# A two-layer streaming encoder in float32: the second layer's panels computed without the meta-token columns that no output depends on

## The reference

```
def trunk_layer(x, pos, attend, sc_hist, cf_hist, ffn_hist, p):
    xn = rmsnorm(x, p['norm1_g'])
    q, k, v, sc_b, sc_c, sc_h, cf_a, cf_gate, gate_pre = jnp.split(xn @ p['w_in'], IN_SPLITS, axis=-1)
    ...
    y_attn = y_attn @ p['w_attn_out']
    sc_conv, new_sc = causal_dwconv(sc_c * sc_h, sc_hist, p['sc_conv_w'])          # width 3
    y_sc = (sc_b * sc_conv) @ p['w_sc_out']
    glu = cf_a * jax.nn.sigmoid(cf_gate)
    cf_conv, new_cf = causal_dwconv(glu, cf_hist, p['cf_conv_w'])                  # width 31
    y_cf = jax.nn.silu(layernorm(cf_conv, p['cf_ln_g'], p['cf_ln_b'])) @ p['w_cf_out']
    g_attn, g_sc, g_cf = jnp.split(jax.nn.sigmoid(gate_pre + p['b_gate']), 3, axis=-1)
    x = x + (g_attn * y_attn + g_sc * y_sc + g_cf * y_cf) @ p['w_o']
    h = rmsnorm(x, p['norm2_g']) @ p['w_up']
    h, new_ffn = causal_dwconv(h, ffn_hist, p['ffn_conv_w'])                       # width 3
    hg, hu = jnp.split(h, 2, axis=-1)
    return x + (jax.nn.silu(hg) * hu) @ p['w_down'], ...

y_prompt = rmsnorm(xp, final_g)[:, N_META:]        # the 16 meta tokens are dropped
y_sample = rmsnorm(xs, final_g)
```

## Time and profile before

| | us |
|---|---|
| median of 3 runs | 2459.11 (2457.91 to 2459.72) |
| profiled execution, its own time | 2460.99 |
| span of its trace, first to last instruction | 2459.7 |
| TensorE busy | 2390.1 (97%) |
| VectorE busy | 1616.4 (66%) |
| ScalarE busy | 891.3 (36%) |
| TensorE's granted clock, mean | 0.992 of full speed |

### The profile page before, as it was taken

One profiled execution on the slowest core, in us unless ns is written; L12 is line 12 of the kernel. 1 busy time (PEld: TensorE's weight loads), 2 busy tenths in 40 slices (PEclk: granted clock), 3 DMA queues, 4 the chain that ended last, 5 costly groups with the idle time before them and its releaser, 6 DMA issues.

```text
span 2459.7 us, 41837 instructions
## 1 busy us (share of the span) xinstructions
PE 2390.1 (97%) x17698; PEld 2342.4 (95%) x17698; DVE 1616.4 (66%) x2393; ACT 891.3 (36%) x1704; POOL 41.5 (2%) x73
## 2 busy tenths in 40 slices
PE   7999999999999999999999999999999999999997
PEld 6988899999999999999998889999999999999996
DVE  6577698895535664645764777988864356556366
ACT  4355322223523432423434562222244234234243
POOL 2000000000000000000010000000000000000000
PEclk9999999999999999999999999999999999999998
DMA  5311222222332222222242112222223322222222
GB/s 195 93 44 52 65 78 86 79 78 78 96 103 88 81 78 81 83 78 86 90 141 69 52 45 75 85 78 86 78 78 95 100 86 79 85 78 85 79 78 93
DMA packets 58284, 206.30 MB, mean 84 GB/s; under 512 B 8494, under 2 KB 8590, under 8 KB 57838
## 3 DMA queue, kind: packets, MB, share of 16 engines
q1 hardware_dynamic: 54704, 191.56, 24.0%
q0 software_dynamic: 3392, 12.05, 1.7%
HBM read 192.09 MB, written 8.50 MB: 82 GB/s over the span
## 4 chain that ended last, share of the span: by engine, by line
PE 89%; DVE 6%; ACT 2%; issue 2%; DMA 0%; SPq 0%; DVEq 0%; ACTq 0%
PE ps L386 86%; DVE cf_acc L1016 1%; PE ps L430 1%; DVE w_lo L825 1%; PE ps L443 1%; PE ps L462 1%; ACT w_hi L574 1%; PE ps L466 0%; DVE xn_hi_lo L873 0%; PE ps L398 0%; ACT scratch L657 0%; ACT L651 0%; ACT L601 0%; DVE scratch L869 0%; PE ps L448 0%
## 5 line engine op out<-in xcount | busy, mean ns | idle before, releaser
L386 PE MATMUL ps<-xn_hi_lo,w_hi 128*128 128x304 f32 (+1 forms) x7552 | 1358.5, 302 | 20.6 <-DVE w_lo L825 12.8
L386 PEld LDWEIGHTS ps<-xn_hi_lo,w_hi 128*128 128x128 f32 x7552 | 1122.7, 189 | 39.2 <-issue 27.3
L386 PE MATMUL ps<-xn_hi_lo,w_lo 128*128 128x304 f32 x3776 | 821.9, 299 | 0.0
L825 DVE TENSOR_TENSOR w_lo<-raw,w_hi 128x1024 fp32r<-128x1024 f32 x348 | 426.2, 1225 | 543.2 <-ACT w_hi L574 543.2
L574 ACT ACTIVATE w_hi<-raw 128x1024 fp32r<-128x1024 f32 x348 | 369.0, 1060 | 1121.2 <-PE ps L386 1120.7
L386 PEld LDWEIGHTS ps<-xn_hi_lo,w_lo 128*128 128x128 f32 x3776 | 609.2, 189 | 0.0
L386 PE MATMUL ps<-branch_hi_lo,w_hi 128*128 128x304 f32 (+1 forms) x2944 | 523.1, 300 | 3.8 <-DVE branch_hi_lo L1161 1.6
L386 PEld LDWEIGHTS ps<-branch_hi_lo,w_hi 128*128 128x128 f32 x2944 | 436.2, 188 | 6.7 <-DVE branch_hi_lo L1161 2.1
L1016 DVE SCALAR_TENSOR_TENSOR cf_acc<-glu,vec,cf_acc 128x622 f32<-128x622 f32 x480 | 382.8, 861 | 0.0
L386 PE MATMUL ps<-branch_hi_lo,w_lo 128*128 128x304 f32 x1472 | 318.9, 298 | 0.0
L386 PEld LDWEIGHTS ps<-branch_hi_lo,w_lo 128*128 128x128 f32 x1472 | 236.1, 188 | 0.0
(11 more groups left out here) (123 smaller groups left out, 1293.2 us busy)
## 6 DMA issues: line engine op xcount, KB each, us to landing
raw<-in_weights SPq DMA_DIRECT2D x348, 512.0 KB, 3.4
spill<-x_q_merged POOLq DMA_DIRECT2D x2, 2368.0 KB, 9.4
x_q_merged<-spill POOLq DMA_DIRECT2D x16, 296.0 KB, 3.2
x_q_merged<-in_xt SPq DMA_DIRECT2D x4, 592.0 KB, 8.7
out_y<-x_q_merged SPq DMA_DIRECT2D x8, 296.0 KB, 2.2
scratch<-scratch SPq DMA_DIRECT2D x72, 18.5 KB
scratch<-scratch SPq DMA_DIRECT2D x8, 132.0 KB, 2.3
con<-in_consts SPq DMA_DIRECT2D x1, 592.0 KB, 12.1
```

What stands on the lines that cost most here:

```text
L386: last = nc.tensor.matmul(to[:, t0:t1], a[:, w % 2, wk], both[:, part, k, t0:t1], start=(k == 0 and j == 0), stop=(k == nk - 1 and j == 2))
L825: V.tensor_tensor(wl[:, w % 2, :], raw[:, w % 2, :], f(wh[:, w % 2, :]), ALU.subtract).then_inc(lo_done, 1)
```

## The change

A function `lead(l, n)` gives, for each panel, the number of leading columns that are left out. In the first layer and ahead of the first gate panel it is 0. Behind that it is 16 for the down-projections, 12 for the short convolution's C and h panels, whose product the width-3 convolution reads two columns back, and 14 for all others. The front half's matmul and the operations of ScalarE and VectorE that read a panel out of PSUM or make its successor's input start at that column. Taps, layer norm, the feed-forward's convolution and SiLU, the channel sums and the final norm keep all columns. Number and order of the instructions on each engine, the semaphores and the transfers are as before.

```diff
--- before.py
+++ after.py
@@ -116,6 +116,19 @@
 
 
 USES = tile_uses()
+
+
+def lead(l, n):
+
+    if l < DEPTH - 1 or n < N_OA:
+        return 0
+    if N_SC <= n < N_OS and (n - N_SC) % 3 < 2:
+        return N_META - 2 * S_H
+    return N_META if any(p0 + 2 * k <= n < p0 + 2 * k + KT for t0, k, p0 in PARTS) else N_META - S_H
+
+
+def pieces(first):
+    return (first, TP - first), (TP, DEC_SEQ)
 
 
 def after(t0, hist):
@@ -382,7 +395,7 @@
                 pe.wait_ge(lo_done, w + 1)
             wk, to = slice(k * 128, k * 128 + 128), ps((l, n))
             for j, (a, part) in enumerate(((wh, 0), (wh, 1), (wl, 0))):
-                for t0, t1 in ((0, FRONT), (FRONT, TOK)):
+                for t0, t1 in ((lead(l, n), FRONT), (FRONT, TOK)):
                     last = nc.tensor.matmul(to[:, t0:t1], a[:, w % 2, wk], both[:, part, k, t0:t1],
                                             start=(k == 0 and j == 0), stop=(k == nk - 1 and j == 2))
             if k == nk - 1:
@@ -598,7 +611,8 @@
         def gate(l, n, j, bias):
 
             act.wait_ge(panel_done, l * PANELS + n + 1)
-            nc.scalar.activation(slot(O_SG, TOK, j), ps((l, n)), ACT.Sigmoid, bias=bias) \
+            t = lead(l, n)
+            nc.scalar.activation(slot(O_SG, TOK, j)[:, t:], ps((l, n))[:, t:], ACT.Sigmoid, bias=bias) \
                 .then_inc(out[USES[(l, n)][0]], 1)
 
         for m in range(KT):
@@ -717,11 +731,13 @@
                 if m >= 2:
                     tile_emptied(act, (l, n - 5))
                 act.wait_ge(panel_done, W + n + 1)
-                nc.scalar.activation(slot(O_CT, TOK, m % 2), ps((l, n)), ACT.Copy).then_inc(out[USES[(l, n)][0]], 1)
+                t = lead(l, n)
+                nc.scalar.activation(slot(O_CT, TOK, m % 2)[:, t:], ps((l, n))[:, t:], ACT.Copy).then_inc(out[USES[(l, n)][0]], 1)
                 high(W + n + 3)
                 high(W + n + 4)
                 tile_emptied(act, (l, n + 2))
-                nc.scalar.activation(bh[:, m, :], slot(O_BT, TOK, m % 2), ACT.Copy).then_inc(sc_hi, 1)
+                t = lead(l, n + 2)
+                nc.scalar.activation(bh[:, m, t:], slot(O_BT, TOK, m % 2)[:, t:], ACT.Copy).then_inc(sc_hi, 1)
 
             def mean(m):
                 act.wait_ge(sum_ps, l * 4 + 2)
@@ -767,7 +783,8 @@
                 high(W + N_OC + 2 * m + 3)
                 act.wait_ge(mg_done, l * 16 + 8 + m + 1)
                 act.wait_ge(tails_out, l * 32 + 32)
-                nc.scalar.activation(mh[:, m, :], X[:, m, :], ACT.Copy).then_inc(mg_hi, 1)
+                t = lead(l, N_WO)
+                nc.scalar.activation(mh[:, m, t:], X[:, m, t:], ACT.Copy).then_inc(mg_hi, 1)
             residual(l, N_WO, (l, l * 27 + 18, "g2"))
             root(l * 4 + 4, (l, "n2"), TOK, O_RF)
             act.wait_ge(ff_zero, l * 4 + 4)
@@ -842,11 +859,12 @@
             V.scalar_tensor_tensor(xl[:, m, :], X[:, m, :], col(l, g, m), f(xh[:, m, :]), ALU.mult, ALU.subtract) \
                 .then_inc(nx_lo, 1)
 
-        def conv3(src, dst, l, name, t, signal, base):
-            V.tensor_scalar(dst, src[:, 0:S_OUT], col(l, name, t * 3), None, ALU.mult).then_inc(signal, 1)
+        def conv3(src, dst, l, name, t, signal, base, first):
+            dst = dst[:, first:]
+            V.tensor_scalar(dst, src[:, first:S_OUT], col(l, name, t * 3), None, ALU.mult).then_inc(signal, 1)
             for k in (1, 2):
                 dve.wait_ge(signal, base + k)
-                V.scalar_tensor_tensor(dst, src[:, k:k + S_OUT], col(l, name, t * 3 + k), dst, ALU.mult, ALU.add) \
+                V.scalar_tensor_tensor(dst, src[:, first + k:k + S_OUT], col(l, name, t * 3 + k), dst, ALU.mult, ALU.add) \
                     .then_inc(signal, 1)
 
         zero_sum(O_SS, TOK)
@@ -1032,7 +1050,8 @@
                 low(W + N_OA + 2 * m + 3)
                 tile_emptied(dve, (l, N_OA + 2 * m))
                 dve.wait_ge(panel_done, W + N_OA + 2 * m + 2)
-                V.tensor_tensor(X[:, m, :], slot(O_SG, TOK, m % 2), ps((l, N_OA + 2 * m + 1)), ALU.mult) \
+                t = lead(l, N_OA)
+                V.tensor_tensor(X[:, m, t:], slot(O_SG, TOK, m % 2)[:, t:], ps((l, N_OA + 2 * m + 1))[:, t:], ALU.mult) \
                     .then_inc(out[USES[(l, N_OA + 2 * m + 1)][0]], 1)
                 taps(3)
 
@@ -1048,7 +1067,7 @@
                 low(W + n + 3)
                 tile_emptied(dve, (l, n))
                 dve.wait_ge(panel_done, W + n + 2)
-                for t0, w_ in PIECES:
+                for t0, w_ in pieces(lead(l, n + 1)):
                     o = after(t0, S_H)
                     last = V.tensor_tensor(ch[:, o:o + w_], slot(O_CT, TOK, j)[:, t0:t0 + w_],
                                            ps((l, n + 1))[:, t0:t0 + w_], ALU.mult)
@@ -1056,24 +1075,27 @@
                 tile_emptied(dve, (l, n + 1))
                 V.tensor_copy(sct[:, m, 0:S_H], ch[:, TP:TP + S_H])
                 V.tensor_copy(sct[:, m, S_H:2 * S_H], ch[:, S_IN - S_H:S_IN]).then_inc(sc_tail_done, 1)
-                conv3(ch, cv, l, "scw", m, sc_tap, (l * KT + m) * 3)
+                conv3(ch, cv, l, "scw", m, sc_tap, (l * KT + m) * 3, lead(l, n + 2))
                 taps(2)
                 low(W + n + 4)
                 dve.wait_ge(panel_done, W + n + 3)
                 dve.wait_ge(sc_tap, (l * KT + m) * 3 + 3)
-                for t0, w_ in PIECES:
+                for t0, w_ in pieces(lead(l, n + 2)):
                     o = t0 + (S_H if t0 >= TP else 0)
                     last = V.tensor_tensor(bt[:, t0:t0 + w_], cv[:, o:o + w_], ps((l, n + 2))[:, t0:t0 + w_], ALU.mult)
                 last.then_inc(out[3], 1)
                 taps(2)
                 dve.wait_ge(sc_hi, l * KT + m + 1)
-                V.tensor_tensor(bl[:, m, :], bt, f(bh[:, m, :]), ALU.subtract).then_inc(sc_lo, 1)
+                t = lead(l, n + 2)
+                V.tensor_tensor(bl[:, m, t:], bt[:, t:], f(bh[:, m, t:]), ALU.subtract).then_inc(sc_lo, 1)
 
             def merge(m, n, nth):
                 j = m % 2
-                V.tensor_tensor(slot(O_TQ, TOK, j), slot(O_SG, TOK, j), ps((l, n)), ALU.mult).then_inc(out[USES[(l, n)][0]], 1)
+                t = lead(l, n)
+                V.tensor_tensor(slot(O_TQ, TOK, j)[:, t:], slot(O_SG, TOK, j)[:, t:], ps((l, n))[:, t:], ALU.mult) \
+                    .then_inc(out[USES[(l, n)][0]], 1)
                 tile_emptied(dve, (l, n))
-                V.tensor_tensor(X[:, m, :], X[:, m, :], slot(O_TQ, TOK, j), ALU.add).then_inc(mg_done, 1)
+                V.tensor_tensor(X[:, m, t:], X[:, m, t:], slot(O_TQ, TOK, j)[:, t:], ALU.add).then_inc(mg_done, 1)
 
             def tile_sum(m):
                 ss = view(O_LS, CF_OUT)
@@ -1132,7 +1154,8 @@
                 dve.wait_ge(panel_done, W + n + 2)
                 merge(m, n + 1, 8)
                 dve.wait_ge(mg_hi, l * KT + m + 1)
-                V.tensor_tensor(ml[:, m, :], X[:, m, :], f(mh[:, m, :]), ALU.subtract).then_inc(mg_lo, 1)
+                t = lead(l, N_WO)
+                V.tensor_tensor(ml[:, m, t:], X[:, m, t:], f(mh[:, m, t:]), ALU.subtract).then_inc(mg_lo, 1)
 
             def residual(n0, following=None):
                 for m in range(KT):
@@ -1140,7 +1163,9 @@
                     if following is None or following[2] == "g2":
                         if n0 == N_WO:
                             dve.wait_ge(x_back, l * (KT * 16) + m * 16 + 16)
-                    V.tensor_tensor(X[:, m, :], X[:, m, :], ps((l, n0 + m)), ALU.add).then_inc(out[USES[(l, n0 + m)][0]], 1)
+                    t = lead(l, n0)
+                    V.tensor_tensor(X[:, m, t:], X[:, m, t:], ps((l, n0 + m))[:, t:], ALU.add) \
+                        .then_inc(out[USES[(l, n0 + m)][0]], 1)
                     low(W + n0 + m + 2)
                     if following is not None:
                         nl, q, g, hi = following
@@ -1166,7 +1191,7 @@
                         .then_inc(ff_tap, 1)
 
                 def scaled(dst, key):
-                    for t0_, w_ in PIECES:
+                    for t0_, w_ in pieces(lead(*key)):
                         o = after(t0_, S_H)
                         last = V.tensor_tensor(dst[:, o:o + w_], view(O_RF + t0_, w_), ps(key)[:, t0_:t0_ + w_], ALU.mult)
                     last.then_inc(out[USES[key][0]], 1)
```

## The result

The changed kernel took 2444.16 us (median of 4 runs, 2442.09 to 2445.80) against 2459.41 (4 runs, 2457.91 to 2460.74): a ratio of 0.9938, 95% interval 0.992 to 0.9955, 15.3 us less. The two profiled executions, 2460.99 and 2442.09, are 18.9 us apart.

What follows compares the result with a forecast made beforehand. TensorE, busy 97% and never waiting in key second-layer stages, was taken as the bound. Dropped columns save 20.6 us, less 0.60 and 0.45 given back: 19.5 off 2459.1 gives 2439.6 us, range 2437 to 2444.

Steps and rivals of the forecast that it cites:

- the other engines' share: ScalarE and VectorE: their narrower operations are worth nothing outside the named waits, since they wait on TensorE.
- VectorE stays below the bound of the short convolution: Second layer's short convolution: against the rival that VectorE (88% busy) becomes the bound, giving 2442.6 us; rival's chance 6%.
- a sum of 19.5: Whole kernel: 20.6 us of dropped columns less 0.60 and 0.45 given back, 19.5 us saved.
- the spread of the runs: Range of the forecast time: 1.2 us, taken as the runs' distance below the median, widening the range only downwards.
- Columns on TensorE, 20.6 us: Second layer's front-half matmuls: 49344 columns dropped in 3504 matmuls, at 1 / 2.4 ns a column, save 20.6 us.
- Size it is: TensorE's matmuls: time goes by columns, not position, from channel sums of 406, 418, 430 ns at 288, 304, 318 columns.
- The Trainium skill's slope between its sustained gaps: TensorE's matmuls with weight loads: 81 ns at 128 columns, 131 at 512, 0.13 ns a column, implying 6.4 us saved.
- The rival of the starts: 2976 front halves starting off a 64-byte boundary pay for it; at 12.8 ns each 2477.7 us; taken as nothing, chance 5%.
- Given back, 1.05 us: Places where TensorE waits for unshortened work of other engines: 0.60 us behind the short convolution and 0.45 at small places.
- The wait at panel 70: End of second layer's short convolution: TensorE's wait for w_lo grows 0.60 us, from 0.5 to 1.1, after 0.1 from VectorE's narrowing.
- the five ramps: Starts of w_o, first up-projection and three down-projections: 0.28 us more waiting together, plus 0.12 in the last down-projection.
- TensorE's wait in the attention stage: First gate panel: the 2.7 us wait of the last attention block's transposes for branch_hi_lo grows by 0.05 us.

Runs made afterwards that it cites:

- experiment 4: Kernel before with only ScalarE's and VectorE's operations narrowed (rounding of merged branches excepted), matmuls at full width: 2462.50 us against 2461.36, ratio 1.0002.
- 8: Changed kernel with six Conformer taps (twelve VectorE operations) moved into short-convolution tiles 1 to 6: 2441.03 us; the kernel before took 2461.36, ratio 0.9917.

## Why the prediction was right and wrong

*The mechanism was right, the range was not.* TensorE sheds columns where it never waits, the other engines' share is nothing (experiment 4), VectorE stays below the bound of the short convolution. Over 14 and 33 runs the saving is 19.4 us for a sum of 19.5. Part of that agreement is luck: the steps as the traces show them come to 19.0, below. The step that put the measured 2444.16 outside 2437 to 2444 is the term for the spread of the runs, last in this section.

*Columns on TensorE, 20.6 us.* The sum of what the traces show is close: a pair lost 5.4 ns with 14 columns dropped, 7 with 16 (272.2 to 265.2), 6.6 with 12 in the short convolution (from the mean distances of the starts there, 134.2 + 131.4 ns). 2592 x 5.4 + 384 x 6.6 + 528 x 7.0 = 20.2 us. But the agreement hides two errors of opposite sign. Fourteen columns were worth 5.4 ns and not 5.8, sixteen and twelve 7.0 and 6.6 instead of 6.7 and 5.0. A step that failed in kind, though it cost the sum little, is "Size it is": the earlier trace rows are straight over three sizes in plain float32, all read from multiples of 16 columns, and I took from them a straight line for any size and start. The Trainium skill's slope between its sustained gaps ("TensorE: Matmul & The Clock Gate", "Back-to-back issue gap"), 0.13 ns a column, is not borne out: from 304 to 290 columns the trace gives 5.4 / 14 = 0.39.

*The rival of the starts* was priced at a fixed part for every front half off its boundary, and set at nothing because VectorE's taps don't care. The runs show something between: a start at 14 columns costs 288 columns 2.7 ns over a start at 0, and 290 columns nothing; a start at 12 makes 292 columns 1.6 to 2.6 ns cheaper than from 0. VectorE's reads say nothing about TensorE's. The Trainium skill's section "Operand start alignment" (page "SBUF — State Buffer") is about which starts are allowed, and left open just this.

*Given back, 1.05 us.* The wait at panel 70: 0.60 forecast, 0.52 by the idle times (0.34 to 0.86), and the 0.1 for VectorE's own columns came out as 0.11. The distance of the starts at the five ramps grew by 0.05, 0.07, 0.12, 0.12 and, in the last down-projection, 0.06 + 0.14 + 0.06: 0.6 us where 0.40 stood. TensorE's wait in the attention stage rose from 2.67 to 2.75, 0.08 for 0.05. That is 1.2 us for 1.05, and 20.2 less 1.2 is 19.0, beside the 18.9 and 19.1 between traces with like half-clock stretches (experiments 4 and 8). The prediction also misread the level of the wait at panel 70: the 0.5 us of its row are two waits, 0.34 at panel 70 and 0.16 elsewhere, as its own 33.0 less 32.7 us says. So the wait became 0.86 and not 1.1; the growth, which is what the sum uses, wasn't touched by this.

*The step that failed: the spread of the runs.* The 2439.6 stood on a median of three runs, 2459.1, that is 2.8 us below the median of 33; and the four runs of the changed kernel came 1.7 us above that of 14. For the spread the range had 1.2 us, the distance from the lowest of three runs to their median, and only downwards; upwards it had the price of a column and more waiting. The trace had the reason for more: stretches at half clock, which the profile's mean of 0.992 counts. Measured, 7 us lie between fastest and slowest run of either kernel, and three measurements of the same difference gave 15.3, 20.3 and 20.6 us. By my estimate a difference of two medians of three or four runs moves by 3 to 4 us. The median of the 33 runs less 19.5 is 2442.4, and with that spread the upper end comes to about 2446, without any rival. That the first measurement's 4 us are such a draw fits the clocks of the changed kernel's four runs, which carry 1.7 of them; the 2.5 of the kernel before stay open, as the clocks of its first runs weren't recorded.

## What to carry to other kernels

Where TensorE never waits, price dropped columns at one a cycle for the sum, but try the neighbouring sizes and starts before fixing one: here dropping 12 columns beat dropping 14 by 3.5 us (4.7 in the traces), and dropping 16 shortened no stage further. When the bound engine gets faster, look along the chain for the stretches of other engines that it was just covering, and fill their idle time earlier in the program; twelve operations a layer moved into a wait removed 1.1 us in the second layer and 1.0 in the first. Before a forecast of less than 1% is set against medians of three runs, read the mean clock of each and compare runs with like clocks.

## What the hardware showed unexpectedly

- A pair of fp32r matmuls of 292 + 288 columns takes 265.2 ns when the 292 are read from column 12, 266.7 or more from 0, 268.7 from 4. Where the result is written made no difference between 12 and 0; 288 columns read from 16 took 265.2 ns written to 16 and 264.4 written to 0.
- 290 columns from column 0 or 14 cost as much as 292 from column 0, 266.7 to 266.9 ns; from column 12 they took 266.2.
- In 11 of the 12 traces TensorE fell to 1.2 GHz around the end of the attention, in one layer or the other, in none in both; in the changed kernel's it did so at 1467.4, after a wait of 1.80 us, and again at 1481.1, after one of 2.75. Where it fell behind the second layer's first gate, the stage was 1.5 us longer; over a whole run 0.001 of mean clock went with 1.1 to 1.2 us.
